# Down and output products turned round: tokens stationary, weights moving, residual rows per token

## The reference, cut to what matters

```python
# first block
x = x + mixed @ w_out
h2 = rmsnorm(x, norm_ffn)
x = x + jnp.square(jax.nn.relu(h2 @ w_up)) @ w_down          # w_down: 8192 x 2048
# second block
h = rms_norm(x, g_attn_pre) * (1.0 + scale_a) + shift_a
proj = h @ w_in ...                                          # two attentions, dsa and diff, 1024 wide each
mixed = jnp.concatenate([diff_out, dsa_out], axis=-1) @ w_o  # 2048 x 2048
x = x + gate_a * rms_norm(mixed, g_attn_post)
h = rms_norm(x, g_ffn_pre) * (1.0 + scale_f) + shift_f
ff = (jax.nn.silu(h @ w_gate) * (h @ w_up)) @ w_down         # w_down: 5632 x 2048
x = x + gate_f * rms_norm(ff, g_ffn_post)
```

## Time and profile before

| | us |
|---|---|
| median of 3 runs | 2660.43 (2655.79 to 2664.97) |
| the profiled execution | 2662.46, of which the span of the trace is 2660.7 |
| TensorE busy | 2599.8 |
| VectorE busy | 1828.5 |
| ScalarE busy | 1311.3 |
| mean granted TensorE clock | 0.985 of full |

### The profile page before, as it was taken

One profiled execution on the slowest core, in us unless ns is written; L12 is line 12 of the kernel. 1 busy time (PEld: TensorE's weight loads), 2 busy tenths in 40 slices (PEclk: granted clock), 3 DMA queues, 4 the chain that ended last, 5 costly groups with the idle time before them and its releaser, 6 DMA issues.

```text
span 2660.7 us, 39055 instructions
## 1 busy us (share of the span) xinstructions
PE 2599.8 (98%) x15974; PEld 2301.8 (87%) x15974; DVE 1828.5 (69%) x2629; ACT 1311.3 (49%) x2011; POOL 0.2 (0%) x4
## 2 busy tenths in 40 slices
PE   7999999999999999999998999999899999999997
PEld 6888899988888888888887899998688888888886
DVE  5557548588888788788788658666766656655565
ACT  5456336455554444444445544565544444444445
POOL 0000000000000000000000000000000000000000
PEclk9999999999999999999998999999899999999999
DMA  7555444788878878879786645445377667655552
GB/s 255 190 182 171 133 143 143 253 306 283 273 239 293 282 261 302 274 270 306 255 281 210 205 157 170 144 156 175 124 233 230 214 205 231 213 189 190 190 190 79
DMA packets 335722, 572.16 MB, mean 215 GB/s; under 512 B 16502, under 2 KB 161168, under 8 KB 334776
## 3 DMA queue, kind: packets, MB, share of 16 engines
q1 hardware_dynamic: 301424, 451.58, 51.4%
q10 hardware_dynamic: 34120, 118.09, 12.8%
HBM read 558.01 MB, written 10.49 MB: 214 GB/s over the span
## 4 chain that ended last, share of the span: by engine, by line
PE 95%; ACT 2%; DVE 2%; issue 1%; ACTq 0%; DVEq 0%
PE ps L453 49%; PE ps L454 25%; PE ps L918 3%; PE ps L919 3%; PE ps L920 3%; PE ps L718 3%; PE ps L719 2%; PE ps L720 2%; PE ps L470 1%; PE ps L498 1%; DVE wl L1582 1%; PE ps L780 1%; PE ps L509 0%; PE ps L488 0%; ACT wh L976 0%
## 5 line engine op out<-in xcount | busy, mean ns | idle before, releaser
L1582 DVE TENSOR_TENSOR wl<-raw,wh 128x1024 fp32r<-128x1024 f32 x856 | 1040.2, 1224 | 767.4 <-ACT wh L976 765.1
L976 ACT ACTIVATE wh<-raw 128x1024 fp32r<-128x1024 f32 x856 | 899.7, 1059 | 1143.4 <-PE ps L454 867.7
L453 PE MATMUL ps<-hs,wh 128*128 128x512 f32 x3664 | 1291.0, 397 | 15.0 <-issue 10.5
L454 PE MATMUL ps<-hs,wl 128*128 128x256 f32 x3664 | 1027.0, 280 | 0.0
L453 PEld LDWEIGHTS ps<-hs,wh 128*128 128x128 f32 x3664 | 689.8, 188 | 182.9 <-issue 12.7
L454 PEld LDWEIGHTS ps<-hs,wl 128*128 128x128 f32 x3664 | 693.2, 189 | 0.0
L453 PE MATMUL ps<-ff,wh 128*128 128x512 f32 x1728 | 602.0, 394 | 0.0
L454 PE MATMUL ps<-ff,wl 128*128 128x256 f32 x1728 | 481.0, 278 | 0.0
L453 PEld LDWEIGHTS ps<-ff,wh 128*128 128x128 f32 x1728 | 323.9, 187 | 74.9
L454 PEld LDWEIGHTS ps<-ff,wl 128*128 128x128 f32 x1728 | 325.2, 188 | 0.0
L918 PE MATMUL ps<-hs,wh 128*128 128x256 f32 x640 | 185.6, 290 | 0.0
(11 more groups left out here) (271 smaller groups left out, 1916.6 us busy)
## 6 DMA issues: line engine op xcount, KB each, us to landing
raw<-w_down SPq DMA_DIRECT2D x108, 1024.0 KB
raw<-w_in SPq DMA_DIRECT2D x80, 1024.0 KB
raw<-w_up SPq DMA_DIRECT2D x64, 1024.0 KB
ada_w<-w_ada ACTq DMA_DIRECT2D x96, 512.0 KB, 5.4
ada_more<-w_ada ACTq DMA_DIRECT2D x96, 512.0 KB, 6.3
raw<-w_gate SPq DMA_DIRECT2D x88, 512.0 KB
raw<-w_up SPq DMA_DIRECT2D x88, 512.0 KB
raw<-w_in SPq DMA_DIRECT2D x72, 512.0 KB
```

The costliest lines, as they stand in the source:

```text
L453: nc.tensor.matmul(ps[0:m, b, :], wh[:, slot, w0:w0 + m], x2, start=k == 0, stop=False)
L454: mm = nc.tensor.matmul(ps[0:m, b, 0:T], wl[:, slot, w0:w0 + m], x2[:, 0:T], start=False, stop=end)
L976: nc.scalar.activation(wh[:, h % WH_SLOTS, :], raw[:, slot, HALF * q:HALF * (q + 1)], ACT.Copy).then_inc(wh_ready, 1)
L1582: nc.vector.tensor_tensor(wl[:, h % WH_SLOTS, :], raw[:, slot, HALF * q:HALF * (q + 1)], wh[:, h % WH_SLOTS, :], ALU.subtract).then_inc(wl ...
```

## The change

The down products of both feed-forward parts and the whole `w_o` product are computed by a new `across`: 128 tokens of the activation are the stationary operand and 512 weight columns move, so the result is tokens by features. Per k it issues 6 matmuls of 512 columns (2 token tiles; high x high, high x low, low x high) in place of 8 matmuls (or 12 narrow ones in L8A). The residual becomes rows (`x_rows`, later `x_back`); after `w_out` it is still built transposed and turned by 32 transposes (`x_turn`) inside the first down steps of LF1. A norm is now a sum along the free dimension: ACT squares with a running sum (`row_squares`), DVE reduces 8 numbers, ACT takes the root of 128 x 2, DVE its reciprocal and scales each row by a number per partition. For the next product the normed rows are turned by TensorE (`rows_turn`, 8 groups of 4 transposes, the last 4 groups between halves of the following step), DVE applies gain and shift on the way out of PSUM (`rows_value`), ACT copies the high part, DVE subtracts the low part. The output norms need their gain along the free dimension: the 128 x 16 column gain is written to DRAM element by element and read back broadcast to 128 partitions (`ga_row`, `gf_row`). The output needs no transposes; SP and ACT store 8 pieces. The norm before LF1 and everything up to it are unchanged.

```diff
+            def across(a, p, panels, b, lhs, split=None, after={}):
+                last = 2 * panels - 1
+                for h in range(2 * panels):
+                    slot = (2 * p + h) % WH_SLOTS
+                    if split is not None:
+                        pe.wait_ge(split[0], split[1] + 2 * h + 2)
+                    pe.wait_ge(wl_ready, 2 * p + h + 9)
+                    for i in range(2):
+                        sums = ps[:, b + i, :]
+                        for kk in range(2):
+                            k = 2 * h + kk
+                            hi, lo = lhs(k, i * P), lhs(k, T + i * P)
+                            w = slice(512 * kk, 512 * kk + 512)
+                            nc.tensor.matmul(sums, hi, wh[:, slot, w], start=k == 0, stop=False)
+                            nc.tensor.matmul(sums, hi, wl[:, slot, w], start=False, stop=False)
+                            mm = nc.tensor.matmul(sums, lo, wh[:, slot, w], start=False, stop=k == 2 * last + 1)
+                        if h == last and i == 0:
+                            mm.then_inc(across_done, 1)
+                    mm.then_inc(half_used, 1)
...
+            def rows_turn(f, j):
+                src, b = (a_rows, f_rows)[f], 4 * f + j % 4
+                pe.wait_ge(sem("rows_normed"), 8 * f + j // 2 * 2 + 2)
+                if j >= 4:
+                    pe.wait_ge(sem("hs_value"), ND * f + 2 * (j - 4) + 2)
+                for a in range(2):
+                    for i in range(2):
+                        mm = nc.tensor.transpose(ps[:, b, a * T + i * P:a * T + (i + 1) * P],
+                                                 src[:, i, (2 * j + a) * P:(2 * j + a + 1) * P], ident[:])
+                mm.then_inc(sem("rows_turned"), 1)
...
+            for j in range(4):
+                rows_turn(0, j)
...
-            for i in range(12):
+            for i in range(8):
                 narrow_step(i)
...
+            for s in range(4):
...
+                across(16 + s, L8A.panel + 2 * s, 2, 2 * (s % 2), dsa_part,
+                       after={h: heads_after(88 + 4 * s + h) for h in range(4)})
+            for s in range(4):
...
+                across(20 + s, L8B.panel + 2 * s, 2, 2 * s, diff_part,
+                       split=(sem("hs_lo"), ND * FILL_ATT + 8) if s == 0 else None)
+            for j in range(4):
+                rows_turn(1, j)
...
-            norm_sums(NORM_FF, LF2.step + 34)
-
-            for b in range(8):
...
-                    mm = nc.tensor.transpose(ps[:, b, i * P:(i + 1) * P], xt[:, 4 * q + i, (b % 2) * P:(b % 2 + 1) * P],
-                                             ident[:])
...
         @block.scalar
...
+            def row_squares(i, x, d, ready, n):
+                for r in range(2):
+                    act.wait_ge(ready, n + r + 1)
...
+                    nc.scalar.activation(unused[:, r, :], x[:, r, 512 * d:512 * d + 512], ACT.Square,
+                                         accum_out=row_sq[i][:, 4 * r + d:4 * r + d + 1]
+                                         ).then_inc(sem("row_squared"), 1)
...
+                        if (c, d, h) == (1, 2, 0):
+                            act.wait_ge(sem("gain_ready"), 2)
+                            act.dma_start(row_spill[1].rearrange("(j p) -> p j", p=P), gf, allow_slow_non_contiguous=True
+                                          ).then_inc(sem("row_spilled"), 16)
+                        if (c, d, h) == (1, 3, 0):
+                            act.wait_ge(sem("row_spilled"), 32)
+                            act.dma_start(gf_row[:], row_spill[1:2, :].to_broadcast([P, D])
+                                          ).then_inc(sem("row_loaded"), 16)
...
+            nc.scalar.activation(m8[:, 0, 0:1], eps, ACT.Sqrt)
...
         @block.vector
...
+            def rows_add(a, p_end, b, dst, src, d):
+                for r in range(2):
...
+                    nc.vector.tensor_tensor(dst[:, r, c], src[:, r, c], ps[:, b + r, :], ALU.add
+                                            ).then_inc(across_summed, 1)
...
+            def rows_gain(i, y, row, d, r):
...
+                nc.vector.tensor_tensor(y[:, r, c], y[:, r, c], row[:, c], ALU.mult).then_inc(sem("row_gained"), 1)
...
+            def rows_root(i):
+                dve.wait_ge(sem("row_squared"), 8 * i + 8)
+                nc.vector.tensor_reduce(row_sum[i], row_sq[i].rearrange("p (r d) -> p r d", r=2), AX.X, ALU.add
+                                        ).then_inc(sem("row_reduced"), 1)
+                dve.wait_ge(sem("row_rooted"), i + 1)
+                link(nc.vector.reciprocal(row_root[i], row_root[i]))
...
+                for r in range(2):
+                    nc.vector.tensor_scalar(dst[:, r, c], src[:, r, c], row_root[i][:, r:r + 1], None, ALU.mult
+                                            ).then_inc(sem("rows_normed"), 1)
...
+                    nc.vector.tensor_scalar(ts[:, k % 4, :], ps[:, 4 * f + j % 4, (k % 2) * T:(k % 2 + 1) * T],
+                                            gain[:, k:k + 1], shift[:, k:k + 1], ALU.mult, ALU.add
+                                            ).then_inc(sem("hs_value"), 1)
...
+            def rows_fill(f):
+                fill = FILLS[f][5]
+                rows_normed(f, 0)
+                rows_normed(f, 1)
+                rows_value(f, 0)
+                rows_value(f, 1)
+                hs_low(fill, 0)
+                rows_normed(f, 2)
+                rows_value(f, 2)
+                hs_low(fill, 1)
+                rows_normed(f, 3)
+                rows_value(f, 3)
+                hs_low(fill, 2)
...
+            rows_gain(R_FF, ff_rows, gf_row, 3, 0)
+            rows_root(R_FF)
+            rows_gain(R_FF, ff_rows, gf_row, 3, 1)
+            for d in range(4):
...
+                for r in range(2):
+                    nc.vector.scalar_tensor_tensor(out=x_back[:, r, c], in0=ff_rows[:, r, c],
+                                                   scalar=row_root[R_FF][:, r:r + 1], in1=x_back[:, r, c],
+                                                   op0=ALU.mult, op1=ALU.add).then_inc(sem("row_updated"), 1)
```

More of the change, by code:

```diff
@@ L432, in _, with step @@
         def _(pe):
-            def step(p, dp, t, dt, tiles, rhs, panels=4, split=None, between=None):
+            def step(p, dp, t, dt, tiles, rhs, panels=4, split=None, after={}):
                 pe.wait_ge(tile_summed, 4 * (t + dt) + 4)
@@ L477, in from_hs @@
                 return hs[:, k, :]
[L479 to L495, removed]
-                            pe.wait_ge(sem("squared"), 4 * k + 4)
-                        for i in range(4):
-                            mm = nc.tensor.matmul(ps[:, bank(t, 0), 0:T], ones[:], squares_of(k)[:, j, i, :],
-                                                  start=(j == 0 and i == 0), stop=(j == 1 and i == 3))
-                    mm.then_inc(sem("norm_summed"), 1)
@@ new lines, in ff_part, with ffn_sums @@
+            def ff_part(k, c0):
+                return ff[:, k, c0:c0 + P]
+            def ffn_sums():
+                pe.wait_ge(tile_summed, 4 * (LF1.step + 1) + 4)
+                pe.wait_ge(sem("squares_folded"), 2)
+                for j in range(2):
+                    if j:
+                        pe.wait_ge(sem("squared"), 4)
+                    for i in range(4):
+                        mm = nc.tensor.matmul(ps[:, bank(LF1.step + 1, 0), 0:T], ones[:], sq_first[:, j, i, :],
+                                              start=(j == 0 and i == 0), stop=(j == 1 and i == 3))
+                mm.then_inc(sem("norm_summed"), 1)
@@ L755, in _, with x_turn @@
-            ffn_chunk(0, first=True)
-            for c in range(1, 4):
+            def x_turn(q):
+                pe.wait_ge(tile_summed, 4 * (LF1.step + 4) + 8)
+                if q:
+                    pe.wait_ge(sem("x_copied"), 2 * q)
+                for i in range(2):
+                    for n in range(4):
+                        mm = nc.tensor.transpose(ps[:, 2 + i, n * P:(n + 1) * P], xt[:, 4 * q + n, i * P:(i + 1) * P],
+                                                 ident[:])
+                    mm.then_inc(sem("rows_turned"), 1)
@@ new lines, in _ @@
+            for s in range(6):
+                gated(LF2.panel + 96 + 4 * s, LF2.step + 16 + s, (32, 2 * s))
+            nc.scalar.activation(m8[:, 0, 0:1], eps, ACT.Sqrt)
+            for d in range(4):
+                p = LF2.panel + 120 + 3 * d
+                for h in range(6):
+                    feed(2 * p + h + 4, 0)
+                    if d and h == 1:
+                        row_squares(R_FF, ff_rows, d - 1, across_summed, 46 + 2 * d)
+            row_squares(R_FF, ff_rows, 3, across_summed, 54)
```

712 lines of the change are left out of this document (393 added, 319 removed).

## The result

The changed kernel takes 2619.49 us (median of 4 runs, 2612.47 to 2622.50), against 2658.11 us (2653.54 to 2664.97) of the kernel before in the same session: ratio 0.9845, 95% interval 0.9819 to 0.9872. The forecast was 2620. The profiled execution took 2622.36 us with a span of 2620.6; the one of before took 2662.46. The difference of the two profiled executions, 40.1 us, is what the traces have to explain; the prediction's sum was 40.7.

The account below looks back on a forecast made before the run. TensorE, busy 98% of the span, was taken as the bound. Gains 15.3 + 3.5 + 12.9 + 12.0 - 3.0 = 40.7 us off 2662.46 gave 2621.8; the median, 2.0 lower, 2620, range 2606 to 2633.

Parts of the forecast that it names:

- Steady products: Down products and `w_o`: equal columns in fewer instructions, 6 per k instead of 8 or 12, gain 15.3 us.
- instruction price: TensorE streams: each warm matmul costs 0.0133 us beyond its columns, whatever its width; 512 columns take 0.2267 us.
- price per column: Rival for TensorE streams: surplus goes by columns, products gain 1.3 us instead of 15.3, total 2634 us; chance 0.22.
- slow stretches: L8B and first chunk of LF2, pairs at 0.353 us against 0.347 in fast ones; 512-column matmuls there some 0.230.
- x_turn: 32 transposes inside the first down steps of LF1: 0.095 us each, 3.0 us more on TensorE.
- LF1 to L7: Border with a norm: TensorE starts at 10.4 us, 5.0 sooner, less 1.5 for 16 turns; net gain 3.5 us.
- L8B to LF2: Border between two products: 19.1 us in place of 33.5, ACT's squares setting the pace; gain 12.9 us after turns.
- The tail: After the last copy to the span's end: 12.0 us in place of 24.0, gain 12.0 us.
- The clock rival: Turns at the borders hold back full clock for a whole step: 33 us lost, total 2653 us; chance 0.08.
- The element-wise store: Slower rival: `gf` written in 4-byte pieces, 9 us hidden or 149 us, total then 2736 us; two slow cases together 0.05.
- Which speed a stretch has: Unchanged wide steps at fast or slow speed: 10 us either way, covered by no rival.

Follow-up runs that it names:

- run 1: On the changed kernel, every 512-column matmul of `across` issued as two of 256 columns: 2653.90 us, ratio 0.9991 to the kernel before.
- run 4: On the changed kernel, the last weight feed before each border moved behind the norm's work, in L8B the gains ahead of the feed: 2617.84 us, ratio 0.9852.
- run 6: On the kernel before, 16 unused transposes put behind the ones-matmuls of both borders: 2660.18 us, measured once.
- run 7: On the kernel before, 48 unused transposes behind the ones-matmuls of both borders, reaching up to the next product: 2664.07 us, measured once.
- run 8: On the kernel before, 16 float32 products of `ones` by `ones` behind the norm sums of both borders: 2649.85 us, measured once.
- run 2: On the changed kernel, wide halves except a step's last issue eight 512-column matmuls, then eight of 256, instead of pairs: 2614.61 us, ratio 0.984.

## Why the prediction was right

*Steady products.* Right in mechanism and nearly in size: the distance is the 0.2267 that the instruction price gave, and the gain 14.1 us where 15.3 stood. The price per column is excluded by the distances and by run 1. Two details were off. The 0.230 for slow stretches never came: the 512-column stream has one lasting speed. And the two halves of `w_o` together gave 1.3 instead of 3.3, since the clock fell there:

```profile
1792.66 4.62 PE L561 MATMUL ps<-rstd,spread 20*128 20x256 f32 x16
1797.21 0.80 PE L474 MATMUL ps<-wh,hs 128*128 128x512 f32 x1
...
1798.66 0.63 PE L474 MATMUL ps<-wh,hs 128*128 128x512 f32 x1
```

From the end of 16 matmuls of 20 rows on, the product ran at half clock up to 1802 (granted clock 0.57 over 1795 to 1803), 0.427 between two starts; some 3 us lost. That is a matter of the run and not of the change. The same 16 matmuls in the trace of the kernel before left the clock full, as in run 4:

```profile
1803.81 0.39 PE L918 MATMUL ps<-hs,wh 128*128 128x256 f32 x1
```

but in the other eight of the ten traces, those of runs 6, 7 and 8 on the kernel before among them, it was 0.50 there for 3.4 to 6.8 us. The trace of before escaped what most pay.

Two slips of the working changed nothing: the stretches called fast "from the second chunk of LF2 on" are its down steps (its up steps, 2200 to 2250 us in the earlier trace rows, are slow), and the column price would give L8A 32 x (1.440 - 1.387) = 1.7 us, not 1.3.

*x_turn.* 3.0 forecast, 3.5 measured; eight turns take about 0.9 us, 0.11 each, not 0.095.

*LF1 to L7.* The gap came out as 10.1, against 10.4, and its steps nearly as written (adds done at 3.7 us against 3.9, root at 5.2 against 5.4). The term that was mis-sized is what follows: 1.5 us were charged for the turns in the next step and nothing credited for the clock. The half-clock stretch shrank from 5.9 to 1.2 us, and the first step of L7 with its 16 turns takes 0.4 us less than before, not 1.5 more.

*L8B to LF2.* 17.7 us against 19.1. "ACT squares at 0.82, so ACT sets the pace" failed: 0.63 and 0.19 were added as if they ran one after the other, but ACT can start a square 0.61 behind the last. DVE sets the pace: its eight updates take 5.4 us here, and in the tail too, with no squares beside them. The cold stretch of 4.0 us vanished, and the up steps with their 16 turns take 0.5 us less than before. In the changed kernel no wait for `wl` stands in either first step, as it does in runs 7 and 8, so the warm start stays whole; what spares it that wait was not tested.

*The tail.* 11.0 against 12.0: the updates take 0.66 each in a row, not 0.69, and the last store 2.7, not 3.6.

*The clock rival* went the other way. Turns that lead into the product held the clock (run 7: no half clock) or woke it (changed kernel: half clock for 1.2 and 0 us more, run 4: 0.2 and 1.3). At the LF2 border of the changed kernel only 13.5 us of idle time and the 16 turns, at granted clock 0.50, lay ahead of the rise, so turns alone raised it. Idle time of 3.0 us or more before the product went with half clock in it (before, run 6); 1.7 us didn't (run 8). The Trainium skill says in "TensorE: Matmul & The Clock Gate", Part 4: PE-mode transpose, that full clock doesn't engage for transposes, since such a transpose "doesn't count as PE-busy the same way". These traces don't show that: 4.8 us of transposes at granted clock 1.00 (run 7).

*The element-wise store* took 13.1 us, against the 74 from which that rival decides and near the 9 us of the bound spread over all engines.

*Which speed a stretch has* was kept in the range (10 us either way) and cost 5.6 us here. That the sum came out within 0.6 us is partly luck: the borders gave 6.7 us more than forecast, and unchanged products took most of it back. Run 2 shows where the two speeds come from, the alternation of the two widths, and the traces show when a speed changes, at an interruption; what picks fast or slow is not settled.

## What to carry to other kernels

In a stream of matmuls count instructions as well as columns: here each costs 13 ns on top of its columns, so let the longer operand move in 512s, and check the reading on two widths before trusting it. Turn the data so that a norm is a sum along the free dimension, and what stands between two products shrinks from ones-matmuls and reciprocals of 256 columns to a few short instructions; then move the feed of later work behind the norm, and let TensorE's turns lead straight into the product, since idle time there can cost twice, once as itself and once as half clock (in the kernel before, most of the second came back as a wait for the feed). Before crediting or blaming a change for a few microseconds, compare the unchanged stretches of both traces.

## What the runs showed of the hardware

- A stream of 512 and 256 columns in turn runs at 0.347 or 0.353 us a pair, at full clock, and keeps its speed until it is interrupted (116 of 117 rows of over 20 pairs); which of the two changes from run to run. Streams of one width have one speed (0.2267 for 512 in `across`, 0.120 for 256).
- Behind eight matmuls of 256 columns the first five of 512 start 0.232 us apart, the next three 0.2267 (run 2).
- ACT squares of 512 columns with a running sum can start 0.61 us apart, though the two records of one are 0.61 and 0.18.
- 16 turns behind 13.5 us of idle time ran at granted clock 0.50, and the clock was full as the product behind them began (changed kernel, LF2).
- 4.8 us of nothing but transposes stayed at full clock (run 7); with 3.0 us of idle time behind 16 of them the product started at half clock (run 6).
- A DRAM write of 2048 single floats landed after 13.1 us.
